# RWKV scan of a two-block kernel: sums and right sides moved ahead of level four, the substitution split, first outputs on ScalarE, small loads on GpSimd's queue

## What is computed

```python
def step(S, inp):
    r_t, w_t, k_t, v_t, kk_t, b_t = inp
    sa = jnp.einsum('bhij,bhj->bhi', S, -kk_t)
    S = (S * w_t[:, :, None, :] + sa[..., None] * b_t[:, :, None, :]
         + v_t[..., None] * k_t[:, :, None, :])
    return S, jnp.einsum('bhij,bhj->bhi', S, r_t)

y = (rwkv7_scan(r_h, heads(decay[:, :, 0]), k_h, v_h, kk, b_h, False)
     + rwkv7_scan(r_h, heads(decay[:, :, 1]), k_h, v_h, kk, b_h, True))
```

## Time and profile before

| | |
|---|---|
| median of 3 runs | 3677.14 us |
| the profiled execution | 3670.67 us |
| its span in the profile | 3669.4 us |
| granted TensorE clock, mean | 0.939 |
| busy over the whole span | PE 3288.6 us (90%), PE weight loads 2729.0, DVE 2274.6 (62%), ACT 995.2 (27%), POOL 369.3 (10%) |
| the scan | about 692 to 1136 us of the span |

### The profile page before, as it was taken

How to read it: one execution, slowest core, us unless ns; L and a number is a source line. 1 busy time by engine, 2 the same in 40 slices (tenths; PEclk the granted TensorE clock), 3 DMA queues, 4 the chain that set the end, 5 groups by cost and what they waited for, 6 DMA issues and landing times.

```text
span 3669.4 us, 56666 instructions
## 1 busy us (share of the span) xinstructions
PE 3288.6 (90%) x24667; PEld 2729.0 (74%) x24667; DVE 2274.6 (62%) x3148; ACT 995.2 (27%) x1468; POOL 369.3 (10%) x202
## 2 busy tenths in 40 slices
PE   6988799788886799999999897998988989999996
PEld 4777667687875578888888676876766778888885
DVE  5758556677774444444444566996555656666666
ACT  4544144311111231111111443113544221112112
POOL 2520033200001200000000121000001001111110
PEclk9989698899997899999999998999999989999999
DMA  4410064212112111111111202113001111111111
GB/s 134 122 47 14 18 186 127 73 34 40 34 29 105 58 46 52 35 52 52 52 52 41 86 35 70 47 48 81 1 1 58 35 40 47 46 46 58 46 46 63
DMA packets 261536, 207.20 MB, mean 56 GB/s; under 512 B 86968, under 2 KB 223943, under 8 KB 260775
## 3 DMA queue, kind: packets, MB, share of 16 engines
q1 hardware_dynamic: 221351, 176.82, 16.1%
q10 hardware_dynamic: 39936, 26.75, 2.7%
HBM read 172.06 MB, written 29.64 MB: 55 GB/s over the span
## 4 chain that ended last, share of the span: by engine, by line
PE 69%; DVE 18%; ACT 6%; POOL 2%; issue 2%; DMA 2%; SPq 1%; ACTq 0%; DVEq 0%; POOLq 0%
PE ps L2034 22%; PE ps L2049 16%; PE ps L1897 5%; PE ps L641 3%; PE ps L642 3%; PE ps L643 3%; PE ps L2782 2%; DVE Yc L2659 2%; DVE s_Z L1639 2%; DVE s_tmp L1638 2%; PE ps L2758 2%; PE ps L1479 2%; POOL a_x L2409 1%; PE ps L2768 1%; PE ps L2759 1%
## 5 line engine op out<-in xcount | busy, mean ns | idle before, releaser
L3076 DVE TENSOR_TENSOR H<-H,ps 128x1024 f32<-128x1024 f32 x256 | 312.7, 1221 | 181.0 <-PE ps L2049 174.1
L2199 DVE TENSOR_TENSOR fsum<-fsum,ps 128x1024 f32<-128x1024 f32 x168 | 205.2, 1221 | 311.6 <-PE ps L2049 309.6
L2049 PE MATMUL ps<-dh,hh 128*128 128x512 f32 x864 | 339.4, 393 | 20.3 <-DVE hl L2014 14.3
L2049 PE MATMUL ps<-dl,hh 128*128 128x512 f32 x864 | 338.1, 391 | 0.0
L2049 PE MATMUL ps<-dh,hl 128*128 128x512 f32 x864 | 337.9, 391 | 0.0
L2034 PE MATMUL ps<-hn_h,uh 128*128 128x512 f32 x704 | 275.5, 391 | 7.0 <-DVE ul L1738 4.6
L2034 PE MATMUL ps<-hn_l,uh 128*128 128x512 f32 x704 | 274.9, 390 | 0.0
L2034 PE MATMUL ps<-hn_h,ul 128*128 128x512 f32 x704 | 274.8, 390 | 0.0
L2034 PE MATMUL ps<-hx_h,uh 128*128 128x512 f32 x512 | 200.5, 392 | 8.4 <-DVE hx_l L2014 5.3
L2049 PEld LDWEIGHTS ps<-dh,hh 128*128 128x128 f32 x864 | 163.3, 189 | 58.7 <-DVE hl L2014 16.0
L2034 PE MATMUL ps<-hx_h,ul 128*128 128x512 f32 x512 | 199.9, 390 | 0.0
(11 more groups left out here) (472 smaller groups left out, 7589.6 us busy)
## 6 DMA issues: line engine op xcount, KB each, us to landing
aw<-in_w_ada_dram ACTq DMA_DIRECT2D x96, 256.0 KB, 3.0
uw<-in_w_mlp_dram SPq DMA_DIRECT2D x32, 512.0 KB, 4.2
dw<-in_w_mlp_dram SPq DMA_DIRECT2D x32, 512.0 KB, 5.1
uw<-in_ffn_gate_dram SPq DMA_DIRECT2D x22, 512.0 KB, 3.9
uw<-in_ffn_up_dram SPq DMA_DIRECT2D x22, 512.0 KB, 5.3
dw<-in_ffn_down_dram SPq DMA_DIRECT2D x22, 512.0 KB, 5.9
cw<-in_w_in_dram SPq DMA_DIRECT2D x20, 512.0 KB, 3.9
o_w<-in_w_out_dram SPq DMA_DIRECT2D x16, 512.0 KB, 13.0
```

What stands on the lines that cost most here:

```text
L2049: mm = pe.e.matmul(ps[:, 2 * pair + hf, :], v[s][:, blk(t)], w[:, half(hf)], start=(m == 0), stop=(m == 2))
L2199: return dve.c.tensor_tensor(f, f, new, ALU.add) if g else dve.c.tensor_copy(f, new)
L3076: return dve.c.tensor_tensor(h, h, self.ps[:, 4 + 2 * (t % 2):6 + 2 * (t % 2), :], ALU.add)
```

## The change

- **PE.** The cumulative sums (u even) move from between l4 and p5 to ahead of p4, behind the transposes. The right sides of a step are no longer at the head of its own pass. They are issued in the pass before: where that pass has no sums, ahead of p4, otherwise behind l5. The Grams gb(n) wait for t5(u) instead of xt(u); gk(n) still waits for xt(u).
- **DVE.** The products for u+3 are split by direction: one before t4, one between t4 and zz. The substitution of step n is split in three: the identity copy and pivots 0 and 1 between zz and t5, pivots 2 to 4 between t5 and xt, pivots 5 to 14 and the last copy behind xt. The wait for N16 stands behind the identity copy. Scaling comes right after the masked Grams.
- **Outputs.** In steps 0 to 7 the output is the first one written to its chunk, and ACT copies it out of PSUM into B. In steps 8 to 15 DVE adds as before, now behind the scaling.
- **Queues.** ACT issues no DMA in the scan any more. SP keeps its four loads of ZZ and issues 10 of the 16 loads of N16 (k = 0 to 4), POOL the other four of ZZ and the other six of N16 (k = 5 to 7).

```diff
@@ rwkv_scan_sp
-            self.blocks_there(sp, self.t_n, n, range(0, 8, 2))
+            self.blocks_there(sp, self.t_n, n, range(0, 5))
@@ new, called by rwkv_scan_pe
+    def right_sides_pe(self, u):
...
+        for d in range(2):
+            pe.wait_ge(dve["scaled", u, d], self.pool["zero"])
+            if (u % 2 or u == 0) and (u + 3) // 2 < NBLK:
+                pe.wait_ge(act["Ei", (u + 3) // 2, d])
+            elif u:
+                pe.wait_ge(act["U", u - 1, d])
+            if u:
+                pe.wait_ge(self.yes(u - 1)["y", u - 1, d])
+            self.heads_pe(d, 2, CH, 0, ((lambda l, H: MM[H, l, 0, :], lambda l, H: self.VT[H, tok[l // 4], l % 4, :]),
+                                        (lambda l, H: AR[H, l, 0, :], lambda l, H: S[H, l, :])), "rh", u, d)
+    def yes(self, u):
+        return self.act if u < NSUB // 2 else self.dve
@@ rwkv_scan_pe
+            sums = u % 2 == 0 and (u + 4) // 2 < NBLK
-                            pe.wait_ge(dve["xt", u, d])
+                            pe.wait_ge(dve[("t5", "xt")[w], u, d])
@@ behind the transposes, ahead of p4
+            if sums:
+                if u >= 0:
+                    pe.wait_ge(act["U", u, 1], self.yes(u)["y", u, 1], dve["S", u, 1])
+                else:
+                    pe.wait_ge(act["Ei", 0, 1])
+                self.cum_pe((u + 4) // 2)
+            elif 0 <= m < NSUB:
+                self.right_sides_pe(m)
@@ behind l5
+                if sums and m > 0:
+                    self.right_sides_pe(m)
@@ rwkv_scan_act
-            if 0 <= u + 1 < NSUB:
-                act.wait_ge(self.t_z["out", u + 1], self.pool["zero"])
-                self.inverse_back(act, self.t_zb, u + 1, range(1, 8, 2))
+            if 0 <= u < NSUB // 2:
+                for d in range(2):
+                    tok = self.gla_where(u // 2, u % 2)[d][0]
+                    act.wait_ge(pe["yy", u, d])
+                    act.e.activation(self.B[:, 0:4, tok:tok + CH], self.hb(d, 2), ACTF.Copy).then_inc(*act.one("y", u, d))
...
-                act.wait_ge(self.t_n["out", u + 2])
-                self.blocks_there(act, self.t_nb, u + 2, range(1, 8, 2))
@@ rwkv_scan_pool
+        for n in range(NSUB + 1):
+            if n:
+                pool.wait_ge(self.t_z["out", n - 1], pool["zero"])
+                self.inverse_back(pool, self.t_zb, n - 1, range(1, 8, 2))
+            if n < NSUB:
+                pool.wait_ge(self.t_n["out", n])
+                self.blocks_there(pool, self.t_nb, n, range(5, 8))
@@ substitute_dve(n, first, end)
+        if first == 0:
+            if n:
+                dve.wait_ge(self.t_z["out", n - 1])
+            dve.c.tensor_copy(self.Z16[:, :, 1], self.eye16[:]).then_inc(*dve.one())
+            dve.wait_ge(self.t_n["in", n], self.t_nb["in", n])
...
-        for s in range(15):
+        for s in range(first, end):
@@ rwkv_scan_dve, order of a pass: S, nm, mm, scaled, then
+            if u >= NSUB // 2:
...
+                    dve.wait_ge(pe["yy", u, d], act["y", NSUB - 1 - u, 1 - d])
...
+                products(u + 3, 0)
...
+                products(u + 3, 1)
...
+                self.substitute_dve(n, 0, 2)
...
+                self.substitute_dve(n, 2, 5)
...
-                self.substitute_dve(n)
+                self.substitute_dve(n, 5, 15)
```

More of the change, by code:

```diff
@@ L1490, in cum_pe @@
             mm.then_inc(*pe.one("cum", t, d))
+    def right_sides_pe(self, u):
+        pe, act, dve = self.pe, self.act, self.dve
+        tok = [w[0] // CH for w in self.gla_where(u // 2, u % 2)]
+        S, AR, MM = self.S[u % 2], self.AR[u % 3], self.MM[u % 3]
+        for d in range(2):
[10 more added lines that the diff above has]
+        return self.act if u < NSUB // 2 else self.dve
     def rwkv_scan_pe(self):
@@ L1499, in rwkv_scan_pe @@
                 v = lambda l, H: self.VT[H, tok[l // 4], l % 4, :]
[L1500 to L1508, removed]
             if n < NSUB:
@@ L1615, in rwkv_scan_pool, with substitute_dve @@
     def rwkv_scan_pool(self):
-        self.pool.e.memset(self.S[0][:], 0.0).then_inc(*self.pool.one("zero"))
+        pool = self.pool
+        pool.e.memset(self.S[0][:], 0.0).then_inc(*pool.one("zero"))
+        for n in range(NSUB + 1):
[5 more added lines that the diff above has]
+                self.blocks_there(pool, self.t_nb, n, range(5, 8))
         self.meet(self.pool, "rwkv_scan")
-    def substitute_dve(self, n):
+    def substitute_dve(self, n, first, end):
         dve = self.dve
[L1622 to L1625, removed]
+        if first == 0:
[3 more added lines that the diff above has]
+            dve.wait_ge(self.t_n["in", n], self.t_nb["in", n])
         N, Z = self.N16[:, 0], self.Z16[:, 0, 1]
@@ L1639, in substitute_dve @@
             dve.c.tensor_tensor(rows, rows, part, ALU.subtract).then_inc(*dve.one())
-        dve.c.tensor_copy(self.Z16[:, :, 0], self.Z16[:, :, 1].rearrange("p d i c -> p d c i")).then_inc(*dve.one("x16", n))
+        if end == 15:
+            dve.c.tensor_copy(self.Z16[:, :, 0], self.Z16[:, :, 1].rearrange("p d i c -> p d c i")).then_inc(*dve.one("x16", n))
     def rwkv_scan_dve(self):
@@ L1649, in rwkv_scan_dve, with products @@
             dve.at["scaled", 0, d] = dve.n
-        def products(n):
+        def products(n, d):
             t, AR, F = n // 2, self.AR[n % 3], self.F[n % 3]
[L1653 to L1668, removed]
@@ L1670, in rwkv_scan_dve @@
-        products(0)
+            tok, s = self.gla_where(t, n % 2)[d]
+            tc, W = slice(s * CH, (s + 1) * CH), slice(tok, tok + CH)
+            last = s * CH + (CH - 1 if d == 0 else 0)
+            dve.wait_ge(act["Ei", t, d])
+            if n >= 3:
+                dve.wait_ge(pe["yy", n - 3, d])
+            if n:
+                dve.wait_ge(pe["tr", n - 1, d])
+            dve.c.tensor_tensor(F[:, L[d]], self.last[:, L[d]], self.Ei[:, L[d], last:last + 1], ALU.mult).then_inc(*dve.one())
@@ new lines, in products @@
+            dve.e.tensor_tensor(AR[:, L[d], 0], self.kk[:, :, W], self.Ex[:, L[d], tc], ALU.mult).then_inc(*dve.one())
+            dve.e.tensor_tensor(self.BK[:, L[d], 0], self.bb[:, :, W], self.En[:, L[d], tc], ALU.mult).then_inc(*dve.one())
+            dve.e.tensor_tensor(AR[:, L[d], 1], rkv[:, 0:4, W], self.Ei[:, L[d], tc], ALU.mult).then_inc(*dve.one())
+            dve.e.tensor_tensor(self.BK[:, L[d], 1], rkv[:, 4:8, W], self.En[:, L[d], tc], ALU.mult).then_inc(*dve.one())
+            dve.c.tensor_copy(self.last[:, L[d]], self.Ei[:, L[d], last:last + 1]).then_inc(*dve.one("pr", n, d))
@@ L1671, in rwkv_scan_dve @@
+        for d in range(2):
+            products(0, d)
         for u in range(-2, NSUB):
@@ L1683, in rwkv_scan_dve @@
                                             rep(self.gram_mask[:, d].rearrange("p a b -> p (a b)"), 4), ALU.mult).then_inc(*dve.one(name, n, d))
[L1684 to L1688, removed]
-                    dve.e.tensor_tensor(yv, yv, self.hb(d, 2), ALU.add).then_inc(*dve.one("y", u, d))
-            if u + 3 < NSUB:
-                products(u + 3)
             if u >= 0 and m < NSUB:
@@ L1695, in rwkv_scan_dve @@
                     dve.e.tensor_tensor(Sn[:, L[d]], Sn[:, L[d]], rep_last(self.F[m % 3][:, L[d]], CH), ALU.mult).then_inc(*dve.one("scaled", m, d))
+            if u >= NSUB // 2:
+                for d in range(2):
+                    tok = self.gla_where(u // 2, u % 2)[d][0]
+                    yv = self.B[:, 0:4, tok:tok + CH]
+                    dve.wait_ge(pe["yy", u, d], act["y", NSUB - 1 - u, 1 - d])
+                    dve.e.tensor_tensor(yv, yv, self.hb(d, 2), ALU.add).then_inc(*dve.one("y", u, d))
+            if u + 3 < NSUB:
+                products(u + 3, 0)
             if 0 <= m < NSUB:
```

13 lines of the change are left out of this document (5 added, 8 removed).

## The result

After the change the kernel takes **3641.35 us**, the median of four runs (3640.12 to 3642.51). In the same session the kernel before took 3678.94 (four runs, 3671.06 to 3687.08). The ratio is 0.9911, with a 95% interval of 0.9894 to 0.9928: 0.9% faster.

The account below looks back on a forecast made before the run. Bound: a circle of substitution, memory and levels, no engine full. 13 steps from 26.0 to 23.8 us give 28.6, the last step 0.9; with 0.5 lost, 0.3 gained, 2.7 lost, 26.6 off 3677.1 gives 3650.5; range 3625 to 3705.

Parts of the forecast that it names:

- The sums and right sides ahead of level four: PE: 3.72 us of sums in even steps leave the circle; 1.86 us of right sides are done early every step.
- P: Start of level four's matmuls on PE in a step; by PE's own work forecast at T+7.3.
- T: End of a substitution on DVE, from which the times of a step are counted.
- The split: DVE between the levels: 3.07 us of pivots and copy fill its waits; the substitution ends at P+15.7.
- The outputs on ACT: 0.73 us a step leave DVE for the first eight steps, costed at nothing; three late sums cost 0.5 us.
- c: Cost of one DMA on GpSimd's queue: 0.92 us, the middle between ACT's 0.52 and POOL's 1.33.
- the blocks of s_N decide: At the first pivot, loads of s_N set the step at 23.8 us, against 23.5 for s_ZZ and 23.0 for PE.
- The 2.7 us at the start: Loss on the very first blocks: 6 × 0.92 = 5.5 us on POOL against 2.83 on SP.
- the prediction's own formula: A step is the largest of 23.0 (PE), 19.8+4c (s_ZZ) and 14.6+10c (s_N).
- the fast queue: Rival: GpSimd's queue as fast as ACT's, c up to 0.7, some 41 us off, 3636; chance 0.18.
- The floor of 23.0: PE's row: level five ends at P+7.6, the next P follows 15.4 later, 23.0 us a step whatever the queues do.
- The clock paragraph: Level four's matmuls on PE go from 283 to 218 ns, as the wait before them shrinks to some 0.5 us.

Follow-up runs that it names:

- kernel 12: Kernel after plus 32 filler matmuls between p5 and l5, with the loads of ZZ and N16 back on ACT and none on POOL: 3629.21 us.
- Kernel 3: Kernel after with the whole substitution behind xt again, not split: ratio 0.9941 to before, 24.55 us a step.
- kernel 5: Kernel after with all outputs added by DVE behind the scaling, ACT writing none: 3645.15 us.
- kernels 7 and 8: 7: kernel after, SP loading ZZ before writing NM, 3654.38 us. 8: kernel after, inverse not fetched from step 2 on, ratio 0.9903 to before.
- Kernel 10: Kernel after plus 32 filler matmuls, about 1.15 us, between p5 and l5, repeating p5 into unread PSUM columns: 3630.35 us.
- kernel 2: Kernel after with four loads of ZZ and eight of N16 back on ACT's queue, none on POOL: 3637.84 us.
- kernel 6: Kernel after with all 16 loads of N16 on POOL's queue and none on SP's: 3722.89 us.

## Why the prediction was right, and where not

It gave 3650.5 us, faster, range 3625 to 3705; the kernel took 3641.35. The side and the place are right, and the step, too, came out as forecast (23.75 for 23.8). But it did so for another reason than the prediction gave: two errors cancel, and that they do so to 0.05 us is luck.

**The sums and right sides ahead of level four: right.** The prediction put the PE-bound P at T+7.3. Where PE in the kernel after hardly waits and isn't slowed, it is there: 7.4 at n = 5, with 0.2 us of waiting. In kernel 12 it is 7.1 at n = 1, 3, 5 and 7, with no wait.

**The split: right.** The chain from P to the end of the substitution was forecast at 15.7. It is 15.4 to 15.6 at n = 1, 3, 5, 7, 9 and 11, where the sums stand ahead of level four, 15.9 at n = 2, 4, 6 and 8, 15.5 at the other three, and 15.59 on the mean. Kernel 3, without the split, shows its 0.8 us a step.

**The outputs on ACT: right within what the times can tell** (nothing; kernel 5, but see its waits). The sums that wait for DVE's late outputs stand at two steps, not at three: n = 9 and 11. P is at T+8.1 there where nothing else delays it, 0.8 us late at one step, where the prediction counted 0.5 us for all three together.

**c: the term that was mis-sized.** "I take the middle, 0.92": measured 0.56 for s_ZZ beside ACT's 0.52, and 0.62 for s_N beside ACT's 0.38. The rows nearest in what is done were the ones to follow, though the second is still 1.6 times too low; POOL's 1.33 for a tensor instruction said nothing of a DMA. The prediction gave both kinds of load one price. With it fell "the blocks of s_N decide": POOL's six land at T+10 to T+13.6, and DVE waits for them 0.3 us in all 13 steps. The 2.7 us at the start were another product of c; they came to 0.2. At this c the prediction's own formula gives the fast queue, 23.0 a step and 3636.

**The floor of 23.0 was taken as if nothing stood on it.** The steps lie above it, 0.75 us on the mean, and this is what the high c happened to stand for. The term for s_ZZ was too small as well. At c = 0.56 the formula has it at T+4.1+4c = T+6.3, before PE needs it. But POOL starts its loads at T+2.2 to T+4.0, not at T+2.0, and the last of them lands at T+6.6 to T+8.4; SP's four, which the formula leaves out, land at T+6.4 to T+8.7. For s_N the formula gives T+10.1 at the measured prices, where POOL's last lands at T+10.4 to T+13.6: its six also wait for the write of NM to land. The late s_ZZ held up PE; the late s_N cost DVE 0.3 us, since the first pivot stands at T+12.7 to T+14.3. The 13 steps show three additions to P = T+7.3, read from P and the idle time ahead of it:

- 5.4 us of waits for s_ZZ, 3.6 of them in the steps whose right sides stood behind level five of the pass before. There they hold up states and Grams: DVE waits for PE at T, NM is written 0.5 us later (at T+2.3 or later, for T+1.9), and SP's four loads of ZZ stand behind that write.
- About 5 us of PE at half clock, at n = 3, 6, 7 and 11: P is at T+8.6 to T+8.8 there. The fifth stretch is hidden.
- 0.8 us for the late output at n = 9.

Together 11.2, and the 13 values of P sum to 106.0, which is 11.1 above 13 × 7.3. In kernels 7 and 8 the first can't be had for nothing: with the wait halved or gone, s_N is late in the one and PE, behind stretches at half clock, in both.

DVE in the kernel after, timeline at the head of such a step (T = 919.1), then PE in another, at level five:

```profile
919.01 0.40 DVE L1701 TENSOR_TENSOR s_S<-s_S,ps 128x256 f32<-128x256 f32 x1
919.80 0.42 DVE L1701 TENSOR_TENSOR s_S<-s_S,ps 128x256 f32<-128x256 f32 x1 [0.40 <-PE ps L1479]
920.14 1.28 DVE L1706 TENSOR_TENSOR s_NM<-ps,gram_mask 128x512 f32<-128x512 f32 x2
```
```profile
861.36 1.92 PE L1479 MATMUL ps<-s_ZZ,s_T 64*64 64x64 f32 x32 [1.38 <-DVE s_T L1736]
863.06 0.48 PE L1479 MATMUL ps<-s_VT,s_MM 64*64 64x64 f32 x4
```

**The clock paragraph: half right.** It said that level four's matmuls go back to 218 ns because the wait ahead of them shrinks. They did nearly (227), and the 13 stretches at half clock behind that wait are gone. It overlooked that the same change makes a new wait: the pivots "stand in front of t5", and PE idles 1.2 us for it, 1.4 in the step shown, after 0.7 to 1.1 us of waiting for zz and 1.3 us of p5. Around the end of this idle time the granted clock falls to 0.50 for 3.4 us (the second row of the first fence), in five of the 13 steps: l5 takes 1.92 us where the earlier trace rows have 1.15 for 32 such matmuls, and four right sides 0.48 where they had 0.33. Kernel 10 takes the idle time away and, in these 13 steps, the half clock with it. The same wait without half clock stands in the other eight steps, and the number of stretches around level five differs between kernels with the same PE order: five in after, one in kernel 2, none in kernel 5. (The other stretch of kernel 2 and the one of kernel 5 follow waits of 2.1 and 2.0 us for s_ZZ ahead of level four.) Why the clock falls in some steps and not in others stays open.

**What the prediction read right as signs:** steps of 23 to 24 us, DVE's waits gone, PE's wait for s_ZZ at 0.5 us a step, the scan's end 32.7 us earlier (27 forecast), the rest unmoved. Two were off. POOL's DMAs are 0.56 to 0.62 us apart, not 0.75 to 1. And a sign of being wrong came up once, without effect: at n = 7 the last of SP's ten loads of s_N lands at T+11.9, behind POOL's at T+11.2, and DVE wants them at T+14.

**The sum.** 28.6 + 0.9 − 0.5 + 0.3 − 2.7 = 26.6 was forecast; the profiles show 29.4 + 2.0 + 1.6 − 0.2 = 32.7, with the late sums inside the 29.4. The 6.1 us are, but for rounding, c at the start (2.5), step 14 to 15 (1.1), the steps (1.3 beside the forecast's 28.1) and the end (1.3). The other 3 us between 3650.5 and the median are within the scatter of the runs before.

## What to carry to other kernels

Where an unknown price lies between a row of the same operation on another engine and a row of another operation on the same engine, the same operation was much the nearer here, but only load by load: 0.52 us on ACT and 0.56 on POOL for s_ZZ, 0.38 and 0.62 for s_N, and 1.33 for the other operation. Give each kind of transfer its own price. In a circle of several engines a floor is reached only if everything else is early by more than its scatter; look at what stands just under it, and check by an experiment that removes each in turn. When two errors may cancel, check the terms and not only the sum. When a wait is taken away from TensorE, list all its other waits before saying what the clock will do: the wait that work is moved out of, and the one that it is moved from.

## What was not expected of the hardware

- GpSimd's queue issues loads of 16 KB in 64-byte pieces nearly as fast as ScalarE's, 2.24 us for four (ACT: 2.08). For loads of 4 KB it is slower: 10.05 us for sixteen in kernel 6, 0.63 each, where ACT took 3.01 us for eight, 0.38 each. On GpSimd the smaller load is no cheaper.
- SP's four loads of s_ZZ took 3.31 us to issue in one step and 2.13 in the next (timeline of SP above). Both times the 256 KB write of NM had gone out shortly before on the same queue. In kernel 7, where the loads go first, one lands 2.0 us after its issue instead of 2.6 (median); but POOL's four, on another queue, land in 2.3 instead of 2.7 there, so the order on SP's queue is not shown to be the cause.
- Around an idle time of only 1.2 to 1.4 us between bursts of matmuls the granted clock fell to 0.50 in five of 13 steps and not in the others; with some 1.15 us of matmuls put into it there was no such stretch in the 13 steps, and one in the step behind them, at another wait.
